# Gate and up projections of an fp32 decoder layer in seven block products, with a down projection by token halves

## The reference

```
h2 = rmsnorm(x, norm_ffn_g)
gate = causal_dwconv(h2 @ w_gate, ffn_conv_w) + ffn_conv_b      # w_gate, w_up: 1024 x 2816; three taps over tokens
x = x + (silu(gate) * (h2 @ w_up)) @ w_down                     # w_down: 2816 x 1024
return rmsnorm(x, norm_final_g)
```

## Time and profile before

| | us |
|---|---|
| median of 3 runs | 1492.91 (1487.51 to 1493.18) |
| the profiled execution, its own time | 1493.21 |
| its span in the trace | 1491.4 |
| granted TensorE clock, mean of the core | 0.978 of 2.4 GHz |

### The profile page before, as it was taken

The page is one execution under the profiler, slowest core; times in us unless marked ns, Lnnn a source line. Parts: engine busy times, 40 slices in busy tenths (PEclk is TensorE's granted clock), DMA queues, the critical chain, the costliest instruction groups (busy, mean ns, idle before and its releaser), DMA issues.

```text
span 1491.4 us, 16020 instructions
## 1 busy us (share of the span) xinstructions
PE 1449.6 (97%) x6450; PEld 1123.5 (75%) x6450; DVE 676.1 (45%) x820; ACT 381.5 (26%) x485; POOL 112.2 (8%) x85
## 2 busy tenths in 40 slices
PE   7999999999998999989999999999999999999996
PEld 6788888876555765558888888888888888888884
DVE  6342521395434953245344435354443534444355
ACT  6211201302446034433132121212112121211212
POOL 0011000000101001010001000101000010100013
PEclk9999999699998999999999999999999999999998
DMA  5111021000000020021101111111111111111102
GB/s 205 51 56 56 29 77 49 23 1 3 1 1 5 1 88 1 1 85 59 55 29 57 43 57 57 42 42 56 42 42 56 56 42 42 56 42 42 56 0 113
DMA packets 19972, 67.86 MB, mean 46 GB/s; under 512 B 2232, under 2 KB 3000, under 8 KB 19768
## 3 DMA queue, kind: packets, MB, share of 16 engines
q1 hardware_dynamic: 19548, 66.03, 13.0%
q0 software_dynamic: 384, 1.29, 0.4%
HBM read 63.21 MB, written 4.19 MB: 45 GB/s over the span
## 4 chain that ended last, share of the span: by engine, by line
PE 93%; DVE 3%; DMA 1%; POOL 1%; ACT 1%; issue 0%; SPq 0%; POOLq 0%; DVEq 0%; ACTq 0%
PE PS L337 18%; PE PS L341 18%; PE PS L338 18%; PE PS L1222 9%; PE PS L1316 5%; PE PS L1319 5%; PE PS L1315 5%; PE PS L1133 3%; PE PS L1134 2%; PE PS L1206 2%; PE PS L1207 2%; DVE nmax L846 2%; PE PS L1231 1%; PE PS L1104 1%; PE PS L1115 1%; POOL F L516 1%
## 5 line engine op out<-in xcount | busy, mean ns | idle before, releaser
L337 PE MATMUL PS<-R,wh 128*128 128x512 f32 x1200 | 470.7, 392 | 12.9 <-DVE wl L329 11.3
L338 PE MATMUL PS<-R,wh 128*128 128x512 f32 x1200 | 468.6, 390 | 0.0
L341 PE MATMUL PS<-R,wl 128*128 128x512 f32 x1200 | 371.1, 391 | 0.0
L337 PEld LDWEIGHTS PS<-R,wh 128*128 128x128 f32 x1200 | 226.3, 189 | 61.1 <-DVE wl L329 11.7
L338 PEld LDWEIGHTS PS<-R,wh 128*128 128x128 f32 x1200 | 226.3, 189 | 47.6 <-issue 0.7
L341 PEld LDWEIGHTS PS<-R,wl 128*128 128x128 f32 x1200 | 226.2, 189 | 47.5
L322 ACT ACTIVATE wh<-raw 128x1024 fp32r<-128x1024 f32 x97 | 101.9, 1050 | 262.9 <-PE PS L1319 174.0
L1222 PE MATMUL PS<-raw,PBm 128*65 128x512 f32 x296 | 152.8, 600 | 1.4 <-ACT F L623 0.7
L986 DVE TENSOR_TENSOR F<-PS,F 128x1024 f32<-128x1024 f32 x80 | 97.8, 1223 | 86.6 <-PE PS L1319 86.6
L1316 PE MATMUL PS<-R,wh 128*128 128x512 f32 x320 | 124.5, 389 | 0.0
L1315 PE MATMUL PS<-R,wh 128*128 128x512 f32 x320 | 124.5, 389 | 0.0
(11 more groups left out here) (152 smaller groups left out, 1200.4 us busy)
## 6 DMA issues: line engine op xcount, KB each, us to landing
raw<-in_w_units SPq DMA_DIRECT2D x97, 512.0 KB, 3.4
F<-in_xT SPq DMA_DIRECT2D x16, 512.0 KB, 7.0
outT<-F SPq DMA_DIRECT2D x16, 256.0 KB, 2.1
F<-in_w_cmp SPq DMA_DIRECT2D x1, 2048.0 KB, 7.9
R<-in_cmp_masks POOLq DMA_DIRECT2D x1, 512.0 KB, 4.8
R<-in_alibi_q POOLq DMA_DIRECT2D x2, 160.0 KB, 4.8
masks<-in_masks POOLq DMA_DIRECT2D x1, 288.0 KB, 4.0
R<-R SPq DMA_DIRECT2D x4, 48.0 KB
```

What stands on the lines that cost most here:

```text
L337: nc.tensor.matmul(out, w_h, hi(kt)[:, cols], start=first, stop=False)
L338: nc.tensor.matmul(out, w_h, lo(kt)[:, cols], start=False, stop=False)
L341: last = nc.tensor.matmul(out, w_l, hi(kt)[:, cols], start=False, stop=end)
```

## The change: what it does

**Seven products.** Pair 0 stays as it was. For the pairs 1 to 10, w_gate and w_up are each taken as a matrix of 256 output features by 1024 inputs: 20 matrices. Each is cut in four quadrants of 128 outputs by 512 inputs (4 blocks of 128), the activations in four quadrants B11, B12, B21, B22 of 512 features by 512 tokens. Seven products of quadrants or of sums of quadrants (Strassen's scheme in Winograd's form) give the four quadrants of the result; each product is 4 blocks by 3 matmuls, so 84 in a matrix where two units had 96. S1 to S4 are sums of weight quadrants, made for each matrix by POOL (`sum_of`); T1 to T4 are sums of activation quadrants, made once by POOL (`combine`) and split by ACT and DVE (`split_t`). For them x1 is scaled in place (`scaled`), so x1 itself is first stored to DRAM and loaded again during the down projection. Even matrices use banks 0 to 3, odd ones 4 to 7. Products 1 and 3 share a bank, 0 and 4 another, 2 and 6 a third: product 3 waits until DVE has made U2 out of product 1 and the copy U3 of product 0 (ACT, `snapshot`), product 6 until C22 is made. DVE makes U2, U3, C22, C21 and C12 by additions from PSUM, then multiplies each quadrant by RB (gate) or into silu (up) (`fold`). All of this is 128 x 512. Conv taps and silu stay 128 x 1024.

**Down by token halves.** The gated activations go to DRAM (22 times 512 KB) and come back as 44 half rows. The down projection runs after all pairs: for each half of the tokens, 22 inner tiles outside, output tiles inside, eight PSUM banks accumulating over all 22. In the second half six output tiles run so, the last two come after them, from 44 blocks packed in six units. w_down is loaded and split twice. The sums with x1 (`add_down`) are 16 of 128 x 512. The stage is written out without loops.

In the diff below `n_hi`, `n_lo` are as before, `p_lo` counts split weight quadrants, `p_done` finished products, `t_lo` split activation sums. Helpers not shown: `split_product` (one quadrant or sum, hi on ACT, lo on DVE), `down_split` and `a_split` (the same for a unit of w_down and a half row), `weights_free` and `a_free` (the waits for their slots).

```diff
-N_UNITS = FFN0 + 3 * FT
 RING = 3
+
+
+
+
+PAIRS = FT // 2
+MATRICES = 2 * (PAIRS - 1)
+PAIR0 = FFN0 + 4
+DOWN0 = PAIR0 + 2 * MATRICES
+LAST_D = 2
+LAST0 = DOWN0 + FT
+N_LAST = -(-LAST_D * FT // KT)
+N_UNITS = LAST0 + N_LAST
...
+        PRODUCTS = (("A11", "B11"), ("S2", "T2"), ("S1", "T1"), ("S3", "T3"), ("A12", "B21"), ("A22", "T4"), ("S4", "B22"))
+        PRODUCT_BANK = (0, 1, 2, 1, 0, 3, 2)
...
+            for d in range(KT):
+                if OUT0 + 5 + d < PAIR0:
+                    load(sp, OUT0 + 5 + d, 0, 0, 0)
+                sp.wait_ge(x1_ready, d + 1)
+                sp.dma_start(x1_dram[d], F1[:, X1 + d, :]).then_inc(x1_out, 16)
...
+            for row in range(2):
+                sp.wait_ge(unit_lo, PAIR0 - 2 + row + 1)
+                load_blocks(0, row)
+            for e in range(2):
+                store_a(0, e, e + 1)
+            sp.wait_ge(t_lo, 4 * KT // 2)
+            for row in range(2):
+                load_blocks(1, row)
+            for m in range(2, MATRICES):
+                sp.wait_ge(p_lo, NP * (m - 1))
+                for row in range(2):
+                    load_blocks(m, row)
+                if m % 2:
+                    for e in (1, 0):
+                        store_a(m // 2, e, folded(m // 2, 4 - e))
...
+            for v in range(3, STEPS_DOWN):
+                load_down(v)
+                if v < 2 * FT:
+                    load_a(v)
+                if 6 <= v < 6 + KT:
+                    if v == 6:
+                        sp.wait_ge(p_done, NP * MATRICES)
+                        sp.wait_ge(a_last, 32)
+                    sp.dma_start(x2(v - 6), x1_dram[v - 6]).then_inc(x1_back, 16)
...
+            for k in range(4):
+                pool.wait_ge(xg_ready, k + 1)
+                combine("T1", k, b12(k), ALU.subtract, b11(k), 0)
+            for k in range(4):
+                pool.wait_ge(xg_ready, 4 + k + 1)
+                combine("T3", k, b22(k), ALU.subtract, b12(k), k + 1)
+            for k in range(4):
+                combine("T2", k, b22(k), ALU.subtract, t_raw("T1", k), 4 + k + 1)
...
+            def sum_of(m, j):
+                a = lambda name: block_of(m, name)
+                if j == 1:
+                    pool.wait_ge(blocks_in[m % 2], 32 * (m // 2 + 1))
+                if m:
+
+                    pool.wait_ge(p_lo, NP * (m - 1) + [name for name, _ in PRODUCTS].index(f"S{j}") + 1)
+                elif j == 1:
+                    pool.wait_ge(t_lo, 2 * 4)
+                    pool.wait_ge(t_made, 4 * 4)
+                if j == 1:
+                    nc.gpsimd.tensor_tensor(a("S1"), a("A21"), a("A22"), ALU.add).then_inc(s_made, 1)
+                elif j == 2:
+                    pool.wait_ge(s_made, 4 * m + 1)
+                    nc.gpsimd.tensor_tensor(a("S2"), a("S1"), a("A11"), ALU.subtract).then_inc(s_made, 1)
+                elif j == 3:
+                    nc.gpsimd.tensor_tensor(a("S3"), a("A11"), a("A21"), ALU.subtract).then_inc(s_made, 1)
+                else:
+                    pool.wait_ge(s_made, 4 * m + 2)
+                    nc.gpsimd.tensor_tensor(a("S4"), a("A12"), a("S2"), ALU.subtract).then_inc(s_made, 1)
...
             pool.wait_ge(rn_ready, 1)
-            for f in range(FT):
-                pool.wait_ge(silu_ready, f + 1)
-                nc.gpsimd.tensor_tensor(SA[f % 2], SA[f % 2], RB, ALU.mult).then_inc(sr_ready, 1)
+            spread_silu(1, 0)
+            for k in range(4):
+                combine("T4", k, t_raw("T2", k), ALU.subtract, b21(k), 8 + k + 1)
+            for j in range(1, 5):
+                sum_of(0, j)
+            spread_silu(2, 1)
+            for m in range(0, MATRICES, 2):
+                for j in range(1, 5):
+                    sum_of(m + 1, j)
+                if m + 2 < MATRICES:
+                    for j in range(1, 5):
+                        sum_of(m + 2, j)
+                spread_silu(m + 3, 1)
+                spread_silu(m + 4, 0)
...
+            act.wait_ge(x1_out, 16 * KT)
+            act.wait_ge(n_lo_ready, N_OUT)
+            scaled(0)
+            scaled(1)
             norm_act(act, 2)
+            for k in range(2, KT):
+                scaled(k)
...
+            for k in range(4):
+                split_t("T1", k)
+            split_hi(act, FFN0 + 3, 0, 0, 0)
+            tap(0, 0, 1)
+            for k in range(4):
+                split_t("T2", k)
+            silu(1, 0)
+            for k in range(4):
+                split_t("T3", k)
+            tap(1, 1, 2)
+            for n in range(4):
+                split_product(n)
+            silu(2, 1)
+            for k in range(4):
+                split_t("T4", k)
...
+            for k in range(4):
+                split_t("T1", k)
+            split_lo(dve, FFN0 + 3, 0, 0, 0)
+            first_gate(0)
+            taps(1, 0, 0, 1)
+            for k in range(4):
+                split_t("T2", k)
+            first_up(0)
+            for k in range(4):
+                split_t("T3", k)
+            first_gate(1)
+            taps(2, 1, 1, 2)
+            for n in range(4):
+                split_product(n)
+            first_up(1)
+            for k in range(4):
+                split_t("T4", k)
...
+            def sum_u2(m):
+                dve.wait_ge(p_done, NP * m + 2)
+                dve.wait_ge(s1_made, m + 1)
+                nc.vector.tensor_tensor(U2, PS[:, 4 * (m % 2) + 1, :], U3, ALU.add).then_inc(u2_made, 1)
+
+            def sum_u3(m):
+                dve.wait_ge(p_done, NP * m + 4)
+                dve.wait_ge(u2_made, m + 1)
+                nc.vector.tensor_tensor(U3, PS[:, 4 * (m % 2) + 1, :], U3, ALU.add).then_inc(u3_made, 1)
...
+            for m in range(MATRICES):
+                p = m // 2 + 1
+                for q in range(NP):
+                    n = NP * m + q + 4
+                    if q == 0 and m:
+                        sum_c(m - 1, C12)
+                    if q == 2:
+                        sum_u2(m)
+                    if q == 4:
+                        sum_u3(m)
+                    if q == 6:
+                        sum_c(m, C21)
+                    if n < NP * MATRICES:
+                        split_product(n)
+                    if q == 0 and m:
+                        fold(m - 1, C12)
+                    if q == 4:
+                        sum_c(m, C22)
+                    if q == 5:
+                        fold(m, C22)
+                        fold(m, C11)
+                    if q == 6:
+                        fold(m, C21)
+                    if m % 2 and q in (1, 2):
+                        taps(2 * p + q, 2 * p + 2 - q, 2 - q, folded(p, 2 + q))
+                    if m == MATRICES - 1 and q >= 3:
+                        if q in (3, 5):
+                            down_split(q // 2 - 1)
+                        if q in (4, 6):
+                            a_split(q // 2 - 2)
+            sum_c(MATRICES - 1, C12)
+            dve.wait_ge(c_made, 3 * MATRICES)
+            fold(MATRICES - 1, C12)
...
-                if kt == 5:
+                if kt == 6:
...
+            def product(m, q):
+                n = NP * m + q
+                pe.wait_ge(p_lo, n + 1)
+                left = (gr_ready, a_ready)[m % 2]
+                if m < 2:
+                    if q == 0:
+                        pe.wait_ge(gr_ready, m + 1)
+                        pe.wait_ge(a_ready, m + 1)
+                elif q == 0:
+                    pe.wait_ge(left, folded(m // 2, 2))
+                elif q == 1:
+                    pe.wait_ge(u3_made, m - 1)
+                elif q == 2:
+                    pe.wait_ge(c_made, 3 * (m - 1))
+                elif q == 5:
+                    pe.wait_ge(c_made, 3 * (m - 2) + 2)
+                if q == 3:
+                    pe.wait_ge(u2_made, m + 1)
+                elif q == 4:
+                    pe.wait_ge(s1_made, m + 1)
+                elif q == 6:
+                    pe.wait_ge(c_made, 3 * m + 1)
+                name, bank = PRODUCTS[q][1], PRODUCT_BANK[q]
+                if m == 0 and name[0] == "T":
+                    pe.wait_ge(t_lo, 4 * int(name[1]))
+                out = PS[:, 4 * (m % 2) + bank, :]
+
+                fresh = bank not in PRODUCT_BANK[:q]
+                for k in range(4):
+                    w_h, w_l = (product_slot(w, n)[:, k * P:(k + 1) * P] for w in (wh, wl))
+                    nc.tensor.matmul(out, w_h, operand(name, k, 0), start=fresh and k == 0, stop=False, skip_group_check=not fresh)
+                    nc.tensor.matmul(out, w_h, operand(name, k, 1), start=False, stop=False, skip_group_check=not fresh)
+                    last = nc.tensor.matmul(out, w_l, operand(name, k, 0), start=False, stop=k == 3, skip_group_check=not fresh)
+                last.then_inc(p_done, 1)
+
+            for m in range(MATRICES):
+                for q in range(NP):
+                    product(m, q)
...
+            for h in range(HALVES):
```

(10 more changed lines are left out.)

534 lines of the change are left out of this document (355 added, 179 removed).

## The result

| | before | after |
|---|---|---|
| median, us (range, runs) | 1491.51 (1487.51 to 1493.18, 4) | **1447.53** (1445.36 to 1449.10, 4) |
| profiled execution, its span | 1493.21, 1491.4 | 1445.36, 1443.6 |
| mean granted clock | 0.978 | 0.977 |

The ratio is 0.9709 [0.9692, 0.9726]: 44.0 us faster by the medians, against 1445.4 forecast and a range of 1433 to 1463.

A forecast was written before the change was run, and what follows sets the result against it. TensorE's matmul count times spacing was taken as the bound: 1493.2 - 54.4 (matmuls) + 13.0 (start) + 0.5 (seam) - 6.9 (tail) = 1445.4 us, steady state 0; range 1433 to 1463, held 8 in 10.

The forecast's parts named there:

- What bounds it now, and what it removes: Feed-forward stage: TensorE bounds it by matmul count times spacing; 240 fewer at 0.2267 us give -54.4 us.
- (d): Product 3 waits for U2 in every matrix, with slow clock, making the kernel slower than before: 1502 us; chance 0.03.
- (e): Written-out stage starves the instruction stream, or single-bank chains lose the spacing: +54, 1500 us, nothing won; chance 0.02.
- Steady state: Pairs of matrices: DVE 24.6, ACT 14.2, POOL 16 us fit under TensorE's 38.1; held POOL work costs 0.
- product 3 for U2: Odd matrices: tightest wait, U2 ready at 6.3 us, product 3 beginning at 8.15, 1.8 us to spare.
- The sign that TensorE would be idle only for parts of a us after product 3 of the first matrix: From there to the last tile, TensorE was to show no idle time beyond parts of a us.
- rival (b): POOL stands for every DVE operation, or its loss returns on DVE: 40.6 us a pair, +25, 1470; chance 0.08.
- The start: First products after the norm: late POOL sums and DVE's queue delay product 3; +13.0 us with slow clock, bounds 3 and 18.
- 5.9 + 2.5 + 2.5: Start: TensorE waits for U2 at product 3 (5.9), A11's low part (2.5) and S2's split (2.5).
- The seam and the down stage: Last matrix into down projection: splits and loads hidden under TensorE, steps not DMA-bound; +0.5 us, bounds 0 and 5.
- The tail: Last output tiles: -5.9 us of waits for POOL's squares, root and slow clock, plus -1; total -6.9, bounds -3 and -8.
- the term of 1 us: After the last tile: one square goes in by 4 matmuls, second spread no longer under leftover scales; -1 us.

The follow-up runs named there:

- start_order: Changed kernel with the first quadrant A11 split before T2 and T3, and tile 1's gate, taps and up moved into the first matrix: 1449.81 us, ratio 0.9731.
- new_order: Changed kernel with C22 before the split, A11 before T2's low parts, tile 1's gate, taps and up moved later: 1443.31 us, ratio 0.9693.
- no_spread: Changed kernel with POOL's multiplication of silu by RB cut to one column: 1437.41 us, ratio 0.9637.
- no_sums: Changed kernel with POOL's activation sums T1 to T4 cut to one column each: 1444.06 us, ratio 0.9699.
- c22_first: Changed kernel with C22 made before the next quadrant's split in VectorE's queue: 1445.40 us, ratio 0.9688; run again 1441.37 us, ratio 0.9675.
- the second profile: Profile of the changed kernel run again unaltered on another group's chip: median 1448.49 us, ratio 0.9723, stage 693.8 us.
- tail_sums_off: Kernel before the change with POOL's additions of squares in the last stage cut to one column: 1485.33 us, ratio 0.9975.
- both_orders: Changed kernel with A11 split early, tile 1's work moved into the first matrix, and C22 made before the split: 1444.99 us, ratio 0.9694.
- thin_product: Changed kernel with C22 made before the split and product 5 of every matrix cut to one of four blocks: 1418.47 us, ratio 0.9532.

## Why the prediction was right, and where it was not

**What bounds it now, and what it removes: right.** Matmuls L1743 to L1745 and L1755 to L1757 kept 0.2267 us from start to start, in single-bank chains and in written-out code, so 240 fewer were 54.4 us fewer; rivals (d) and (e) had nothing to go on. The 131 ns a matmul of 512 columns that the Trainium skill gives ("TensorE: Matmul & The Clock Gate", back-to-back issue gap) is not seen in any run here.

**Steady state: wrong, and this is the step that failed.** "I read: POOL stands while DVE works on two SBUF inputs, DVE pays nothing" was half of it. DVE stands too, whenever POOL was first. With the unheld durations, DVE had 24.6 us to do in a pair and POOL about 14.6; in the trace they are busy 31.0 and 19.7. Since both totals stayed below 38.1, it cost little, but it cost in order: product 6 had C22 with 3.3 us to spare by my reckoning, and two held splits ahead of it took 5.2 us instead of 1.4. That is nine of the ten waits, +5.6 us in place of 0: eight of 0.50, and 1.5 in the last matrix, where it was a split of w_down that was held. The tenth, in matrix 1, is in the start below. The tightest wait was not product 3 for U2, as I had it, but this one. The sign that TensorE would be idle only for parts of a us after product 3 of the first matrix failed with it: 1.83 us in matrix 1, 1.25 in the last. It is rival (b) in kind, a loss that returns on DVE, at a fifth of the 25 us that I gave it: I had let it fill the pair to above 38.1, where it only ate slack.

**The start: right in size, wrong in place.** I had the low part of A11 ready 38.3 us into the stage (795.4 against sums at 757.1) and U2 at 54.8. Measured are 44.8 and 54.1 (804.78 + 0.68 - 751.33). So the time by which DVE is through its queue was right within 1 us; what I had wrong is where it is lost. I had POOL held and T2 late (done 23.5 us into the stage; measured 18.0), and DVE waiting for it. In fact POOL ran and DVE was held: 3.1 us in T1's low parts, 4.4 in T3's, 0.9 in a tap. That lies ahead of A11, and TensorE, once it has waited 8.4 us there, arrives at product 3 just behind U2. 5.9 + 2.5 + 2.5 became 8.6, the slow clock 2.3 in place of 1.6, and C22 took 2.0 in matrix 1 in place of 0.5 in matrix 0. Why the size could be right all the same: A11 early gained nothing (start_order, new_order), less work on POOL gained 4.4 us (no_spread) and 2.1 (no_sums), and C22 earlier gained 2.0 (c22_first). So the amount of DVE's work, with its holds, sets most of it. But that 13.3 met 13.0 so closely is luck: terms too large and too small made up for each other, and the second profile has 14.5.

**The seam and the down stage: right.** No wait for a DMA, a split or a bank of TensorE is in the trace between the last product and the tail.

**The tail: right**, -6.9 of -6.9. That POOL's squares are 3.6 of it rests on tail_sums_off; the root's 2.3 are what is left of the 5.9, and the term of 1 us was not tested by itself.

**The sum.** Predicted for the stage -47.8, measured -42.0. The profiled execution, for which the sum was made, took 1445.36 us against 1445.4, and this is luck: the unchanged part happened to be 5.8 us shorter in it. That part varies as much without the change: in the profile of tail_sums_off, whose kernel is the one before up to the tail, it took 750.8 us where the profile before has 757.1. The medians, 2 us off, come from runs of the kernel before that spread over 6 us. The distance of the two totals says nothing of how good the parts are.

## What to carry to other kernels

Work given to GpSimd is not free for VectorE: count operations with two SBUF inputs on VectorE and all of GpSimd's tensor work as one queue, and where a result is awaited, put nothing with two SBUF inputs ahead of it in VectorE's program. Operations that read PSUM can stand beside GpSimd. When a start is late because an engine has too much to do by then, bringing the awaited work forward moves the wait and doesn't shorten it. Where the total fits and one result is late, as with C22, one statement moved can win nearly all of it back: here 6.2 us of the 7.6 that its ten waits cost.

## What the runs showed of the hardware that I had not expected

- Beside a 128x1024 operation of POOL a DVE operation of 0.61 us takes 2.57 us in the mean, in a long series of both. Beside 128x512 it is 1.67.
- A wait of 8.4 us, with the granted clock at 0.70 over it, was followed by about ten matmuls at 0.50, the 1.2 GHz level, and the first product took 5.01 us for 2.72. The waits of 4.1 to 8.4 us in the start of the other profiles had 7 to 11 matmuls 0.43 us apart behind them.
- For shorter waits the profiles differ, also for one and the same wait: 1.83 us in matrix 1 had a clock of 1.00 behind it in one profile of the changed kernel and of 0.55 in the other. Waits of 2.79 (both_orders) and 3.26 us (thin_product) were followed by seven matmuls 0.43 us apart, waits of 3.31 (start_order), 3.38 (new_order), 3.39 and 3.21 us (both_orders) by none. The waits of 0.26 us never were.
- The part of the kernel that no experiment on the stage touched took 750.1 to 757.5 us in the profiles. The difference is in more than one stretch. From 465 to 560 us the granted clock was 0.93 in the profile after, 0.91 in the one before and 0.87 in that of c22_first; the same instructions took 96.0, 98.0 and 100.6 us there. From about 260 to 355 us the same instructions took 94.7, 96.4 and 96.8, and the profile before is 2 us behind the one after already at 50 us. What decides this I didn't find out. It is as large as what the order experiments were after, and only stage lengths, or medians of runs on the same chip, could tell them apart.
